# Order of three helper engines' steps in a fused decoder layer: sample key copies, gate weight split, score biasing

## The reference

```
proj = rmsnorm(x) @ w_in          # q, k, v (12 heads x 64), B, C, H (512), g_a, g_b (1024)
att  = three groups of 4 heads, window/dilation (128,1) (512,4) (2048,16), T5 bias, merged over groups by their softmax sums
b    = B * conv3(C * H)           # conv_state: the last two rows of C * H
m    = sigmoid(g_a) * (att @ w_att_out) + sigmoid(g_b) * (b @ w_conv_out)
x    = x + m @ w_o
x    = x + relu(rmsnorm(x) @ w_ff1)^2 @ w_ff2;   y = rmsnorm(x)
```

## Time and profile before

| what | value |
|---|---|
| median of three runs | 1703.64 us (1700.55 to 1704.92) |
| the profiled execution | 1703.28 us, of it the span 1701.5 us |
| TensorE matmul busy | 1653.5 us, 97% |
| TensorE weight load busy | 1605.7 us, 94% |
| VectorE busy | 672.3 us, 40% |
| ScalarE busy | 472.9 us, 28% |
| GpSimd busy | 73.2 us, 4% |
| mean granted TensorE clock | 0.993 of full speed |
| stage 2, third group | from about 410 to 478 us of the span |
| stage 3 | from about 478 to 685 us |
| stage 4 | from about 687 to 823 us |

### The profile page before, as it was taken

The page is one execution under the profiler, slowest core; times in us unless marked ns, Lnnn a source line. Parts: engine busy times, 40 slices in busy tenths (PEclk is TensorE's granted clock), DMA queues, the critical chain, the costliest instruction groups (busy, mean ns, idle before and its releaser), DMA issues.

```text
span 1701.5 us, 28619 instructions
## 1 busy us (share of the span) xinstructions
PE 1653.5 (97%) x10739; PEld 1605.7 (94%) x10739; DVE 672.3 (40%) x1217; ACT 472.9 (28%) x905; POOL 73.2 (4%) x86
## 2 busy tenths in 40 slices
PE   6999999999999999999999999999999999999997
PEld 6999999888988888899999999999999999999997
DVE  5212223334643444333554344333333333333454
ACT  5212224333533434111322330023201330033212
POOL 0430000000000000000022000000000000000011
PEclk9999999999999999999999999999999999999999
DMA  5524554333257766433111111111111111111112
GB/s 161 153 82 137 165 170 138 99 115 96 72 146 174 177 178 163 146 124 96 50 42 45 50 37 50 49 37 49 38 48 40 47 49 37 49 38 48 40 34 105
DMA packets 229016, 152.07 MB, mean 89 GB/s; under 512 B 23869, under 2 KB 219285, under 8 KB 228968
## 3 DMA queue, kind: packets, MB, share of 16 engines
q1 hardware_dynamic: 200412, 120.32, 25.0%
q10 hardware_dynamic: 26268, 28.31, 4.9%
q0 software_dynamic: 2288, 2.80, 0.7%
HBM read 118.32 MB, written 35.43 MB: 90 GB/s over the span
## 4 chain that ended last, share of the span: by engine, by line
PE 87%; issue 3%; DVE 3%; DMA 2%; ACT 2%; SPq 1%; ACTq 1%; DVEq 0%; POOL 0%
PE bank L625 27%; PE bank L626 27%; PE bank L627 27%; PE bank L760 1%; ACT wh L1031 1%; PE bank L729 1%; PE bank L746 1%; PE bank L686 1%; DMA wr<-in_w_conv_out_dram 1%; PE bank L939 1%; DMA xt<-in_x_prompt_dram 1%; DMA out_dram<-yt 0%; PE bank L828 0%; DMA xp<-in_x_sample_dram 0%; PE bank L840 0%
## 5 line engine op out<-in xcount | busy, mean ns | idle before, releaser
L625 PE MATMUL bank<-xhi,wh 128*128 128x352 f32 (+1 forms) x1104 | 372.1, 337 | 3.1 <-DVE sga L1752 2.6
L626 PE MATMUL bank<-xlo,wh 128*128 128x352 f32 (+1 forms) x1104 | 361.7, 328 | 0.0
L627 PE MATMUL bank<-xhi,wl 128*128 128x352 f32 (+1 forms) x1104 | 361.1, 327 | 0.0
L1408 DVE TENSOR_TENSOR wl<-wr,wh 128x1024 fp32r<-128x1024 f32 (+1 forms) x134 | 179.7, 1341 | 247.4 <-ACT wh L1031 245.4
L626 PE MATMUL bank<-flo,wh 128*128 128x368 f32 (+1 forms) x768 | 251.6, 328 | 0.0
L626 PE MATMUL bank<-hlo,wh 128*128 128x368 f32 (+1 forms) x768 | 251.6, 328 | 0.0
L625 PE MATMUL bank<-hhi,wh 128*128 128x368 f32 (+1 forms) x768 | 250.3, 326 | 0.3 <-DVE rel L1808 0.3
L625 PE MATMUL bank<-fhi,wh 128*128 128x368 f32 (+1 forms) x768 | 250.6, 326 | 0.0
L627 PE MATMUL bank<-hhi,wl 128*128 128x368 f32 (+1 forms) x768 | 250.1, 326 | 0.0
L627 PE MATMUL bank<-fhi,wl 128*128 128x368 f32 (+1 forms) x768 | 250.1, 326 | 0.0
L1031 ACT ACTIVATE wh<-wr 128x1024 fp32r<-128x1024 f32 (+1 forms) x134 | 136.1, 1015 | 357.9 <-PE bank L627 301.6
(11 more groups left out here) (214 smaller groups left out, 1746.2 us busy)
## 6 DMA issues: line engine op xcount, KB each, us to landing
wr<-in_w_ff_dram SPq DMA_DIRECT2D x64, 512.0 KB, 3.6
wr<-in_w_in_dram SPq DMA_DIRECT2D x46, 512.0 KB, 3.9
d_T<-stg ACTq DMA_DIRECT2D x18, 544.0 KB, 2.8
kvc<-in_cache_kv_g_dram SPq DMA_DIRECT2D x16, 512.0 KB, 5.5
kvc<-in_cache_kv_g_dram SPq DMA_DIRECT2D x32, 256.0 KB, 6.1
d_tm<-tm ACTq DMA_DIRECT2D x12, 512.0 KB, 3.7
d_m<-bb ACTq DMA_DIRECT2D x8, 544.0 KB, 3.1
ml<-d_m SPq DMA_DIRECT2D x8, 544.0 KB, 4.1
```

The source lines that it names most:

```text
L625: pe.matmul(bank[c][:, 0:n], wh[st_.p][:, k, :], a, start=(k == 0), stop=False)
L626: pe.matmul(bank[c][:, 0:n], wh[st_.p][:, k, :], b, start=False, stop=False)
L627: last = pe.matmul(bank[c][:, 0:n], wl[st_.p][:, k, :], a, start=False, stop=(k == nk - 1))
L1408: dve.tensor_tensor(wl[st_.p][:, 0:nk, :], wr[st_.p][:, 0:nk, :], f32(wh[st_.p][:, 0:nk, :]), ALU.subtract).then_inc(w_lo, 1)
```

## The change

Five steps are moved; no instruction that computes or moves data is added or removed. In order of the diff: the state transposes of the third group go to bank 7 (they wait for the earlier copies out of bank 7 instead of the score biases), and the wait for the state's copy goes from before the first pair to the first transposes that write bank 7; ScalarE's key copy 0 goes ahead of its split; the split of the next g_a block goes between the sigmoids of chunks 1 and 2; VectorE's bias 1 goes ahead of its split in the third group; VectorE's key copy 1 goes ahead of its split.

```diff
@@ turn_probs (TensorE)
                 else:
+                    if g == 2:
+                        pe.wait_ge(cs_ev, 1)
                     pe.wait_ge(pt_d, i * 4 + (8 * g + j))
@@ before the pairs of group 2 (TensorE)
                 pe.wait_ge(cs_d, 2)
-                pe.wait_ge(s_d, 64)
+                pe.wait_ge(pt_d, 16)
                 for f in range(FC):
-                    last = pe.transpose(bank[3][0:18, f * P:(f + 1) * P], csb[:, f, :], ident[:])
+                    last = pe.transpose(bank[7][0:18, f * P:(f + 1) * P], csb[:, f, :], ident[:])
                 last.then_inc(cs_pe, 1)
-                pe.wait_ge(cs_ev, 1)
@@ sample (ScalarE)
+            keys_act(b, 0)
             split_hi(st0 + 1, KD)
-            keys_act(b, 0)
@@ gate_act (ScalarE)
                 chunk_in(st_, c)
+                if c == 2:
+                    split_hi(st_ + 2, KD)
                 act.activation(col(sga, j, KD, t0, t0 + n), bank[c][:, 0:n], ACT.Sigmoid).then_inc(taken[c], 1)
 
         for p in range(2):
             gate_act(0, p)
-            split_hi(Step(S_GATE + 2 * p + 2), KD)
         with act.Fori(1, 4) as i:
             for p in range(2):
                 gate_act(i, p)
-                split_hi(Step(S_GATE + 2 * p + 2, (4, i)), KD)
@@ before and in the pairs (VectorE)
-                dve.tensor_copy(cst[:], bank[3][0:18, :]).then_inc(cs_ev, 1)
+                dve.tensor_copy(cst[:], bank[7][0:18, :]).then_inc(cs_ev, 1)
...
                 if g == 2:
                     z_terms(f)
+                    bias_scores(g, i, 1)
                 split_lo(st1, KD)
                 prompt_chunk(g, st0, f, 0)
-                bias_scores(g, i, 1)
+                if g < 2:
+                    bias_scores(g, i, 1)
@@ sample (VectorE)
+            keys_dve(b, 1)
             split_lo(st0 + 1, KD)
-            keys_dve(b, 1)
             keys_dve(b, 3)
```

## The result

The changed kernel takes **1698.53 us** (median of 12 runs, 1695.62 to 1701.36), the kernel before 1701.84 beside it (12 runs, 1700.41 to 1705.67). The ratio is 0.9969 with a 95% interval of 0.9960 to 0.9978: 3.7 to 6.8 us less, 5.3 at the middle. The profiled executions are 1703.28 and 1697.02, 6.3 apart, with spans of 1701.5 and 1695.2. Forecast was 9.6 less, 1693.7. So the sign was right and the size too large, by 3.3 us against the profiled execution (on which the sum was made) and by 4.8 against the median, which lies right on the slow edge of the range (1698.5).

A forecast was written before the change was run, and what follows sets the result against it. TensorE's own matmuls were taken as 87% of the last-ending chain, so only its waits counted: 1703.28 - 1.0 - 3.0 - 3.4 - 2.2 = 1693.7 us, range 1690.0 to 1698.5.

The forecast's parts named there:

- State to bank 7: Start of the third group: first scores no longer wait for the state's copy; -1.0 us, bounds 0 and -1.05.
- Bias 1 ahead of the split: Third group, two pairs: TensorE's wait for the scores' bias goes; -3.0 us, bounds 0 and -3.3.
- Key copies: Stage 3, copies ahead of the splits: waits of turned keys' group 3 go; -3.4 us, bounds 0 and -4.8.
- the next bound: Stage 3: VectorE's chain behind the w_conv_out load, taken as fixed, leaves 1.15 us, enough for 0.96 a sequence.
- rival D: Stage 3: earlier key loads delay the w_conv_out load by 3.05 us, +2.0 a sequence; slower, 1709.2 us, chance 0.03.
- rival A: Stage 3 gives nothing: loads landing 1 us later make the sums' wait take over the gain; 1697.1 us, chance 0.20.
- b = 0 and b = 1, nothing: Stage 3's first sequences: b = 0's later scores are covered, b = 1 only moves idle time; 0 us.
- rival B: b = 1: TensorE waits near 2.7 us ahead of the probabilities, its clock falls, +2.0; 1695.7 us, chance 0.20.
- Split between the sigmoids: Stage 4 gates: split starts 0.30 us earlier, shortening seven gates' bank waits; -2.2 us, bounds 0 and -2.7.
- rival C: Stage 4: late third sigmoid holds the third short chunk 0.3 us, so gates gain nothing; 1695.9 us, chance 0.08.
- those named for being right: TensorE's key-copy, st and cst waits vanish, sga about 2, sr 2.5 to 3.5; b = 3, 4 each 0.96 us shorter.
- those for being wrong: Fourth-quarter scores wait over 0.5 us, athi waits for sigmoid, w_conv_out loads mostly over 6 us, stage 3 clock falls elsewhere.

The follow-up runs named there:

- e5: The change in full, with SyncE issuing the next sequence's key loads only once this one's maxima are turned: 1693.0 us.
- e8: e4 with ScalarE's two state stores issued behind stage 2, and in b = 0 alone the key copies behind the splits: 1685.43 us.
- e4: The change in full, with SyncE issuing the w_conv_out load ahead of the combine loads instead of behind them: 1686.83 us.
- e6: The kernel before, with none of the change's edits, and the w_conv_out load issued ahead of the combine loads: 1698.49 us.
- e1: The kernel before with the third group's two edits alone (state transposed into bank 7, bias 1 ahead of the split): 1699.08 us.

## Why the prediction was right or wrong, step by step

**State to bank 7, -1.0: right.** From the transposes to the scores it is 0.53 us instead of 1.65, and no wait for bank 7 or for the copy is left.

**Bias 1 ahead of the split, -3.0: right in the second pair, mis-sized in the first.** The second pair gave its 1.5. The term for the first was -(1.64 - 0.2) and measured -0.3: a wait of 0.95 stayed at the third quarter, and 0.37 came back as a wait of the fourth, for which the text had 0.2. It took `z_terms` to keep its time, 419.2, "held by ScalarE, which does not move up". ScalarE did not keep it either: the issue of `d_st` took 2.01 us instead of 0.34, `z_terms` ended at 419.8 and bias 1 began at 420.44, not 419.5 (the step from one to the other is 0.6 us, where the text had 0.3). In the kernel with this stage's edits alone that issue took 1.23, `z` was 0.8 earlier, and the wait was 0.18. With that spread the term runs from -1.8 to about -2.6.

**Key copies, -3.4: wrong, and this is the main miss.** It measured -0.8 to -1.7, with a spread of 0.8 between executions of the old order. The waits of 0.96 went as described. What failed is the sentence on the next bound: "That chain starts at the values product of b-1 and does not get shorter. It leaves 1.15 us". It took the chain's length as fixed, while the change itself moved up the issue of the key loads, which lengthens it; from issue to split it got 0.9 us longer in b = 3, 1.0 in b = 4 and 1.1 in b = 5. By sequence, b = 3 became 0.2 us shorter instead of 0.96, b = 4 and 5 together 0.7 longer instead of 0.96 shorter, and b = 6, where the load was not late, 0.8 shorter, just as forecast. The text had seen the mechanism, as rival D, and set it aside because "both lie in one queue, the weights first". It had asked the wrong question of it: not whether the delay passes the 2.8 us at which the kernel gets slower, but whether it eats the 1.15 us of room. The result is what rival A said of stage 3 (1697.1, chance 0.20; it names loads that land 1 us later), by rival D's cause at a third of its size. The page of the Trainium skill quoted there (DMA: Bandwidth & Descriptors, Queues, rings and completion order) says in which order descriptors are taken, and that a later one may finish its write before an earlier one. That an earlier load is not slowed by a later one in the same queue was my reading of it. Against that reading, e5 beside the change shows 1.3 us in b = 3 and 1.7 in b = 4 and 5.

**b = 0 and b = 1, nothing: right.** In b = 0 the scores wait 0.8 for a key copy, and e8 shows that this costs nothing. In b = 1 TensorE waits 2.48 us ahead of the probabilities, as rival B said, and the clock falls right there, as rival B also said (a row of the timeline, then busy time by stretch: length, PE, PEld, DVE, ACT, POOL, then the granted clock):

```profile
524.73 0.87 PE L862 MATMUL bank<-ident,xs 128*128 128x128 f32 x3 [2.48 <-ACT xs L1276]
```

```profile
523.00:525.00 2.00, 0.27 (x2) 0.30 (x3) 0.91 (x1) 1.98 (x5) 0.00 (x0) 0.84 1.11 261
525.00:528.00 3.00, 3.00 (x13) 2.92 (x12) 2.67 (x6) 2.32 (x4) 0.00 (x0) 0.54 1.04 174
528.00:531.00 3.00, 2.97 (x19) 2.65 (x19) 2.33 (x7) 0.19 (x2) 0.00 (x0) 1.00 0.36 98
```

The granted clock of 0.54 is the 1.2 GHz level. In the 2 us in which it fell, TensorE was busy for 0.27. The Trainium skill (TensorE: Matmul & The Clock Gate, The HAM clock gate) says that idleness halves the clock, and the trace agrees. But it lasted to about 528, half as long as the "most of" a chunk that the rival priced at 2.0 us, and it cost nothing that shows: b = 1 and 2 together take 54.9 us before (with the longer fall of the earlier trace rows), 54.3 with the change, and 54.5 in the third-group kernel, whose profile has no stretch below 1.00 in stage 3. That kernel waits 2.01 us for `xs` and then 1.39 for `sr` in b = 1; in the change the second wait is gone, so the fall of the clock only filled it. The load sets that stretch, whatever the clock does. It is e4, with the load out of the way, that takes 51.8.

**Split between the sigmoids, -2.2: right.** 2.1 by the table, 2.3 in the kernel with this edit alone; the banks' wait fell to 2.0 us, and rival C's wait of `athi` matmuls does not show. In the profile the third sigmoid runs in the shadow of the split:

```profile
747.17 1.06 ACT L1032 ACTIVATE wh<-wr 128x1024 fp32r<-128x1024 f32 x1 [3.60 <-PE bank L627]
...
748.13 0.46 ACT L1314 ACTIVATE sga<-bank 128x368 f32 x1
...
749.97 0.43 PE L625 MATMUL bank<-xhi,wh 128*128 128x352 f32 x1
```

It is ready at 748.6, when the third short chunk's load starts (748.64), which is the margin of nothing that the forecast read from the earlier trace rows.

**The sum.** By the table: 1.1 + 1.8 + 0.8 + 2.1, and 0.5 ahead of the third group and in b = 0, make 6.3 against 9.6 forecast. 2.6 of the difference are the key copies and 1.2 the first pair. The 0.5 was not forecast, and 0.3 of it lies where nothing was changed; that the miss is not larger is luck by that much.

**The signs.** Of those named for being right, the wait for `cst` is gone, `sga` fell to 2.0, and the scores of b = 0 come 0.7 later; but `sr` grew to 4.4 and not to 2.5 to 3.5, `st` kept 1.3, and b = 3 and 4 did not get 0.96 shorter. Of those for being wrong, the fall of the clock at another place came, and had no price; a load of over 6 us came in b = 1 and 5 alone.

## What to carry to other kernels

When an edit lets one engine run earlier, list every DMA whose issue hangs on that engine's progress, and ask what is in flight in the queue at that moment: the edit that needs 1.15 us of room behind a load can itself make the load late. Two bounds that lie within a microsecond of each other must be moved together: here each alone gave 0.8 and 2.7 us in stage 3, both 9. And a load that gates a chain should be issued ahead of loads with slack: that reordering of SyncE's list was worth about 4.5 us alone (e6) and 11.7 on top of the change, and the best kernels (1685.4 and 1685.6) have both. Last, read more than one profiled execution before a line of waits is believed to a microsecond: two kernels with the same stage 3 differed by 2 us in one such line.

## What the runs showed of the hardware

- A load of 256 KB of weights landed 4.1 to 4.8 us after issue in b = 3 and 4 while the next loads of its own queue were 0.9 us or more behind, and 5.2 to 5.9 with them 0.7 or 0.8 behind. In b = 2 it took 4.2 to 6.0 at 0.7, so the distance is not the only thing that counts. It is not protected by being first: with the loads behind it held back, the kernel is 3 to 5 us faster (e5).
- The issue of one small store by ScalarE (`d_st`, 16 KB) took 0.34 us in four kernels with the old start of the third group, and 1.23 to 2.36 in the six with bank 7. In the four the next issue, a store of `cst`, took 0.88 to 1.03 instead of 0.28. ScalarE's instructions up to there are the same, and in all ten one issue is held and comes free 1.8 to 3.0 us after the first (`d_O`) began. What holds it is open.
- TensorE's clock fell to its 1.2 GHz level in b = 1 from about 511 to 518 us before, and from about 524.5 to 528 with the change. b = 1 and 2 together take 54.9 and 54.3 us, and 54.5 in e1, where the clock does not fall. TensorE's waits for the chain behind the load in b = 1 come to 1.2 us before, 2.5 with the change and 3.4 in e1: the half speed took the place of waiting.
